# A hybrid encoder block on one core: three changed orders, and the softmax scaling moved from GpSimd to VectorE

## The reference, cut to what matters

```
h    = rms_norm(x) ; q|k|v|p = h @ W_in                   # 512 | 128 | 128 | 512 columns
q, k = rms_norm per head of 64
a    = softmax([q k / 8 over own chunk and the one before (64 + 64 keys), sink]) @ v    # 8 heads, 2 kv heads
m    = trailing means of p over 2, 4, 8, 16 tokens, minus p, then a 128x128 map per group
x    = x + concat([a, m]) @ W_out
x    = x + (silu(gate) * val) @ W_down     # gate|val = causal conv(3) of rms_norm(x) @ W_up, 5632 columns
```

## Time and profile before

| | before |
|---|---|
| median of 3 runs | 1780.61 us |
| the profiled execution's own time | 1780.53 us |
| its span (first to last instruction) | 1778.7 us |
| TensorE busy | 1755.8 us |
| VectorE busy | 1310.2 us |
| ScalarE busy | 782.6 us |
| GpSimd busy | 240.6 us |
| mean granted TensorE clock | 1.000 |
| moved by DMA | 342.70 MB, 193 GB/s on average |

### The profile page before, as it was taken

How to read it: one execution, slowest core, us unless ns; L and a number is a source line. 1 busy time by engine, 2 the same in 40 slices (tenths; PEclk the granted TensorE clock), 3 DMA queues, 4 the chain that set the end, 5 groups by cost and what they waited for, 6 DMA issues and landing times.

```text
span 1778.7 us, 23402 instructions
## 1 busy us (share of the span) xinstructions
PE 1755.8 (99%) x8490; PEld 1462.1 (82%) x8490; DVE 1310.2 (74%) x1772; ACT 782.6 (44%) x1413; POOL 240.6 (14%) x270
## 2 busy tenths in 40 slices
PE   7999999999999999999999999999999999999999
PEld 6888888888878888888888888888888888888887
DVE  5645643533569999999998998998997778865874
ACT  4554543533555444444455444444444433333321
POOL 1213212202100000000000000000003033220210
PEclk9999999999999999999999999999999999999999
DMA  9556584586555623423366223223226999976884
GB/s 329 223 214 221 186 315 178 190 308 237 217 195 181 212 77 107 160 78 97 121 231 230 71 84 95 71 83 95 71 83 230 343 340 334 307 260 211 301 287 130
DMA packets 214243, 342.70 MB, mean 193 GB/s; under 512 B 14377, under 2 KB 106737, under 8 KB 214129
## 3 DMA queue, kind: packets, MB, share of 16 engines
q1 hardware_dynamic: 194702, 288.72, 48.1%
q10 hardware_dynamic: 19427, 52.49, 7.5%
HBM read 262.51 MB, written 78.64 MB: 192 GB/s over the span
## 4 chain that ended last, share of the span: by engine, by line
PE 90%; DVE 4%; DMA 2%; ACT 2%; issue 1%; POOL 0%; ACTq 0%; SPq 0%; DVEq 0%; POOLq 0%
PE ps L805 29%; PE ps L806 29%; PE ps L807 29%; DMA rw<-in_w_up_dram 1%; DVE wv L1734 1%; PE ps L964 1%; PE ps L988 1%; PE ps L975 1%; DMA h2T_d<-n 1%; PE ps L1028 1%; ACT xs L1226 1%; DMA raw<-in_w_in_dram 1%; DVE hT_lo L1556 0%; DVE va_lo L1740 0%; POOL ss_q L2030 0%
## 5 line engine op out<-in xcount | busy, mean ns | idle before, releaser
L805 PE MATMUL ps<-va_hi,wv 128*128 128x512 f32 x1232 | 480.0, 390 | 4.2 <-DVE va_lo L1740 3.2
L807 PE MATMUL ps<-va_hi,wv 128*128 128x512 f32 x1232 | 479.4, 389 | 0.0
L806 PE MATMUL ps<-va_lo,wv 128*128 128x512 f32 x1232 | 479.3, 389 | 0.0
L805 PEld LDWEIGHTS ps<-va_hi,wv 128*128 128x128 f32 x1232 | 231.3, 188 | 54.8 <-issue 4.9
L807 PEld LDWEIGHTS ps<-va_hi,wv 128*128 128x128 f32 x1232 | 231.3, 188 | 47.9
L806 PEld LDWEIGHTS ps<-va_lo,wv 128*128 128x128 f32 x1232 | 231.3, 188 | 47.5
L805 PE MATMUL ps<-dt_hi,ds_hi 128*128 128x512 f32 x616 | 239.8, 389 | 0.0
L806 PE MATMUL ps<-dt_lo,ds_hi 128*128 128x512 f32 x616 | 239.7, 389 | 0.0
L807 PE MATMUL ps<-dt_hi,ds_lo 128*128 128x512 f32 x616 | 239.6, 389 | 0.0
L1823 DVE SCALAR_TENSOR_TENSOR cb<-ub,cst,cb 128x1024 f32<-128x1024 f32 x176 | 218.8, 1285 | 8.5 <-ACT cb L1346 8.5
L1346 ACT ACTIVATE cb<-ub,cst 128x1024 f32<-128x1024 f32 x88 | 109.0, 1243 | 142.5 <-DVE ub L1878 89.5
(11 more groups left out here) (170 smaller groups left out, 2737.6 us busy)
## 6 DMA issues: line engine op xcount, KB each, us to landing
dg<-gT_d SPq DMA_DIRECT2D x264, 256.0 KB, 5.4
rw<-in_w_up_dram SPq DMA_DIRECT2D x84, 512.0 KB, 5.0
dw<-in_w_down_dram SPq DMA_DIRECT2D x132, 256.0 KB, 5.5
w_hi<-wA_d SPq DMA_DIRECT2D x54, 512.0 KB, 3.3
w_lo<-wA_d SPq DMA_DIRECT2D x54, 512.0 KB, 5.1
gT_d<-cb ACTq DMA_DIRECT2D x44, 512.0 KB, 2.6
wA_d<-w_hi SPq DMA_DIRECT2D x18, 512.0 KB, 6.1
wA_d<-w_lo SPq DMA_DIRECT2D x18, 512.0 KB, 7.1
```

What stands on the lines that cost most here:

```text
L805: pe.matmul(out_ap, l_hi, r_hi, start=first, stop=False, skip_group_check=True)
L806: pe.matmul(out_ap, l_hi, r_lo, start=False, stop=False, skip_group_check=True)
L807: return pe.matmul(out_ap, l_lo, r_hi, start=False, stop=last, skip_group_check=True)
```

## The change

Four edits:
1. **Second weight split in the head.** `split(1)` moves from after the fourth `hT` tile of block 0 to after the eighth, on ScalarE and on VectorE.
2. **Third maximum in block 0.** VectorE now does, after `win 0`: the inverse of tile 0, then `s` of tile 2, then the inverse of tile 1, then `s` of tile 3. Before, it did both inverses and then both maxima. The semaphore counts of `sm_step` follow (`SM_S0`, `SM_INV0`).
3. **Fourth product's operand.** A new step `va3` makes `va_hi[3]` and `va_lo[3]` ahead of the last block's norm: on ScalarE ahead of `n2sq`, on VectorE ahead of all four `n2sc_last`.
4. **Scaling of the probabilities.** GpSimd's `inv` is gone; `inverse` on VectorE ends with the same multiplication, so VectorE does it tile by tile, in all four blocks.

```diff
@@ order, block 0
-            units("inv", a, (0,))
+            units("inv1", a, (0,))
             units("pin", a + 1, (2,))
-            units("s", a, (2,), (3,))
+            units("s", a, (2,))
+            units("inv1", a, (1,))
+            units("s", a, (3,))
@@ order, end
     units("o", last, (1, 2), (1, 3))
+    units("va3", last, ())
     units("n2sq", last, ())
@@ ScalarE and VectorE, t1
-                    if a == 0 and i == 3:
+                    if a == 0 and i == KT - 1:
                         split(1)
@@ ScalarE
+            def va3(_):
+                act.wait_ge(S["unit_used"], N_UNITS)
+                v_hi(0, 3)
+                v_hi(1, 3)
             def first_up():
-                act.wait_ge(S["unit_used"], N_UNITS)
-                v_hi(0, 3)
-                v_hi(1, 3)
@@ VectorE
             def inverse(a, t):
...
-                dve.wait_ge(S["sm_step"], 12 * a + SM_INV[t])
+                dve.wait_ge(S["sm_step"], 12 * a + (SM_INV if a else SM_INV0)[t])
                 v.reciprocal(row_sum[:, t, :], row_sum[:, t, :]).then_inc(S["inv_ready"], 1)
+                dve.wait_ge(S["inv_ready"], NT * a + t + 1)
+                pr = xs[:, t, :].rearrange("p (i k) -> p i k", i=8)
+                v.tensor_tensor(pr, pr, row_sum[:, t, :].unsqueeze(2).broadcast_to([P, 8, P]), ALU.mult
+                                ).then_inc(S["p_scaled"], 1)
...
+            def va3(_):
+                v_lo(0, 3)
+                v_lo(1, 3)
             def first_up():
                 n2sc_last(0)
                 n2sc_last(1)
-                v_lo(0, 3)
-                v_lo(1, 3)
                 n2sc_last(2)
                 n2sc_last(3)
@@ GpSimd
-            def inv(a, j):
-                for i in (2 * j, 2 * j + 1):
-                    pool.wait_ge(S["inv_ready"], NT * a + i + 1)
-                    pr = xs[:, i, :].rearrange("p (i k) -> p i k", i=8)
-                    g_.tensor_tensor(pr, pr, row_sum[:, i, :].unsqueeze(2).broadcast_to([P, 8, P]), ALU.mult
-                                     ).then_inc(S["p_scaled"], 1)
```

More of the change, by code:

```diff
@@ L1331, in va @@
                 v_hi(c, i)
+            def va3(_):
+                act.wait_ge(S["unit_used"], N_UNITS)
+                v_hi(0, 3)
+                v_hi(1, 3)
             walk(dict(n1=n1_, n1sq=n1sq, t1=t1, pin=pin, pc=pc, pm=pm, kv=kv, kve=kve, q=q, kt=kt, qt=qt, s=s, pt=pt, av=av,
-                      o=o, n2sq=n2sq, t2=t2, first_weights=first_weights, va=va))
+                      o=o, n2sq=n2sq, t2=t2, first_weights=first_weights, va=va, va3=va3))
             def tap2(un, s):
@@ L1680, in inverse @@
                                 ).then_inc(S["sm_step"], 1)
-                dve.wait_ge(S["sm_step"], 12 * a + SM_INV[t])
+                dve.wait_ge(S["sm_step"], 12 * a + (SM_INV if a else SM_INV0)[t])
                 v.reciprocal(row_sum[:, t, :], row_sum[:, t, :]).then_inc(S["inv_ready"], 1)
+                dve.wait_ge(S["inv_ready"], NT * a + t + 1)
+                pr = xs[:, t, :].rearrange("p (i k) -> p i k", i=8)
+                v.tensor_tensor(pr, pr, row_sum[:, t, :].unsqueeze(2).broadcast_to([P, 8, P]), ALU.mult
+                                ).then_inc(S["p_scaled"], 1)
             SM_S, SM_INV = (0, 2, 6, 8), (5, 6, 11, 12)
+            SM_S0, SM_INV0 = (0, 2, 5, 8), (5, 8, 11, 12)
             def s(a, t):
@@ L1696, in s @@
                                 AX.X, ALU.max).then_inc(S["sm_step"], 1)
-                dve.wait_ge(S["sm_step"], 12 * a + SM_S[t] + 1)
+                first = 12 * a + (SM_S if a else SM_S0)[t]
+                dve.wait_ge(S["sm_step"], first + 1)
                 v.scalar_tensor_tensor(shift[:, t, :], mx[:, t, :], -1.0, neg_sink[:], ALU.mult, ALU.min
                                        ).then_inc(S["sm_step"], 1)
-                dve.wait_ge(S["sm_step"], 12 * a + SM_S[t] + 2)
+                dve.wait_ge(S["sm_step"], first + 2)
                 v.tensor_tensor(sink_exp[:, t, :], sink[:], shift[:, t, :], ALU.add).then_inc(S["shift_ready"], 1)
@@ L1809, in first_weights @@
                     lo(0, i)
-            walk(dict(n1=n1_, n1sc=n1sc, t1=t1, win=win, pin=pin, pl=pl, o=o, q=q, qn=qn, kv=kv, kve=kve, join=join, s=s, inv=inv, av=av,
-                      n2sc=n2sc, first_weights=first_weights, va=va))
+            def va3(_):
+                v_lo(0, 3)
+                v_lo(1, 3)
+            walk(dict(n1=n1_, n1sc=n1sc, t1=t1, win=win, pin=pin, pl=pl, o=o, q=q, qn=qn, kv=kv, kve=kve, join=join, s=s, inv=inv, inv1=inverse, av=av,
+                      n2sc=n2sc, first_weights=first_weights, va=va, va3=va3))
             def tap(un, s, j):
@@ L2084, in _ @@
             pool.wait_ge(const_pool, CONST_POOL)
-            walk(dict(n1=n1sq, n1sq=n1sq, n2sq=n2sq, pin=pin, q=q, kve=kve, inv=inv, av=av))
+            walk(dict(n1=n1sq, n1sq=n1sq, n2sq=n2sq, pin=pin, q=q, kve=kve, av=av))
             def keep_halo(un):
```

## The result

| | before | after |
|---|---|---|
| median (15 runs each) | 1780.64 us (1780.05 to 1782.48) | 1785.06 us (1783.85 to 1787.11) |
| the profiled execution's own time | 1780.53 us | 1784.33 us |
| its span | 1778.7 us | 1782.5 us |

The ratio is 1.0025, with a 95% interval from 1.0018 to 1.0031. The changed kernel is slower by 4.4 us, on the side that the prediction gave a chance of 0.11, and outside its range.

The account below looks back on a forecast made before the run. TensorE, busy 99% of the span, was taken as the bound, so only its waits count. Terms -2.6 - 1.3 + 3.5 + 1.75 = +1.35 on 1780.53 gave 1781.8 us, range 1778.4 to 1783.8.

Parts of the forecast that it names:

- the side that the prediction gave a chance of 0.11: Whole kernel: slower than before by more than 0.2% (3.6 us), chance 0.11.
- The four scalings follow: Switch to the second half: scalings right after the `va_lo` pair, last ending at 518.5; part of edit 3's 2.6 us gain.
- The stream is 1.75 us late: Head: later load of weight unit 3 delays unit 5's landing, so TensorE loses 1.75 us at 38.48.
- no GpSimd pass beside it: Block 0, tile 2's 8-column shift: without GpSimd's multiplication alongside it saves 0.7 us, within the 1.3 us gain.
- The rival by which GpSimd's pass is no hindrance: Block 0: the reorder alone moves tile 2's maximum by 1.0, leaving 0.3 to 0.7 of the wait; 1782.4 us, chance 0.07.
- The landing doesn't move: Head: unit 5 lands as before and edit 1 keeps its 0.8 us gain; 1779.3 us, chance 0.17.
- the page cited in the prediction: Head: skill page's DMA cost, estimated 3.2 us for 512 KB; unit 3 lands no later, edit 1 keeps its gain.
- The `hT_lo` halves don't hold TensorE: Blocks 1 and 2: TensorE has two transposes of probabilities in between, so no 3.5 us loss; 1778.4 us, chance 0.08.
- The gain of edit 3 is given back at 591: TensorE's last wait: if `rw` loads pace its chain, TensorE waits 2.6 us longer there; 1784.5 us, chance 0.09.
- the slower rival: At 591: TensorE arrives 2.6 us earlier but waits that much longer for `rw` loads; 1784.5 us, chance 0.09.
- edit 3's bound of 0: Switch to the second half: worst case for the fourth product's operand, no gain; the other bound was -2.9 us.
- edit 1's +2.7: Head: worst case, unit 5's landing moves by the whole delay of unit 3's load, 2.7 us lost.

Follow-up runs that it names:

- order3: Edit 3 alone (fourth product's operand ahead of the norm) on the kernel before: 1780.21 us against 1780.66, ratio 0.9996.
- order3_psum: Kernel before plus edit 3, its two early `va_lo` passes reading their first input from PSUM: 1779.4 us against 1780.73, ratio 0.9991.
- split1: Edit 1 alone (second weight split after the eighth `hT` tile) on the kernel before: 1784.99 us against 1780.66, ratio 1.0022.
- scale4_late: Kernel before plus edit 4, inverses and scalings of tiles 2 and 3 behind the `hT_lo` halves in blocks 1 and 2: 1781.2 us, ratio 1.0004.
- max2: Edit 2 alone (new order in block 0, GpSimd still scaling) on the kernel before: 1780.03 us against 1780.73, ratio 0.9994.

## Why the prediction was wrong, point by point

**Edit 3: the step that failed.** The prediction has "The four scalings follow (0.7 each); the last waits for GpSimd's power near 517.7 and ends at 518.5". The first half, the fourth product, was right (-1.9 forecast by its idle time and restart, -1.76 to -1.93 measured). The power, however, was taken at the times it had before. Beside the moved `va_lo` pair its two steps for tile 0 grew from 0.19 and 0.55 us to 1.26 and 1.41. Then each scaling holds back the next power (0.55 to 0.91), and the four tiles come one every 1.27 us, where 0.7 was counted. The last scaling ends at 520.82 in `order3`, 2.3 later than forecast; the transposes wait 0.71 us and the fifth product 0.93. So -2.6 was forecast and -0.72 (alone) to -0.80 (in the changed kernel) measured. `order3_psum` recovers 1.2 of the 1.9 us that are missing at the switch in `order3`. The remaining 0.7 is the fifth product's wait, which was to vanish and stays (0.61 us in `order3_psum`, 0.60 before). That the scalings and the powers in turn cause it is inferred from their rows; no run takes it apart. The row that should have told me stood in the trace before: the earlier trace rows show a VectorE instruction of 8 columns held for 0.88 us by a GpSimd pass. I used it for block 0 and did not ask where the same thing would happen the other way round. The same trace had that too: beside the scaling that starts at 515.66, GpSimd's power at 515.91 took 0.91 us in place of 0.55.

**Edit 1: the mechanism was right, its size was off, and an effect was missing.** The load's issue was placed within 0.1 us. The term "The stream is 1.75 us late" is mis-sized: the landing of unit 5 moved by 2.72 us, 2.26 without the later start. The forecast let traffic restart at full rate 1.5 us after the issue; it restarted as a ramp (154 and 256 GB/s in the windows from 22 and 23 us, the first more than 1.3 us after the issue), and the hole is 928 KB. The trace before had shown such a ramp behind the load issued at 13.81: 129 GB/s in the window that the earlier trace rows show, then 267 and 428. What makes the ramp was not tested. Edit 1 cost 2.26 us in the changed kernel's profile and 2.03 alone, against 1.75. Not foreseen at all: after the pause of about 3 us TensorE's clock fell to 1.2 GHz in a share of the runs. It does not show in the changed kernel's profiled execution (clock 1.000). As far as the mean clocks of the runs tell, it is why the median lies at 1785.06 and not near 1784.1, where the seven runs at full clock are. In the profiled execution of `split1` it is 2.7 of 4.9 us.

**Edit 4 in blocks 1 and 2: right.** 1.74 us each were forecast, 1.65 and 1.70 measured, 1.69 and 1.72 alone. `scale4_late` shows the reason given to be the cause: with the same passes behind the halves the loss is gone.

**Edits 2 and 4 in block 0: the sum was right, one reason was not needed.** -1.3 forecast, -1.31 measured. But the 0.7 us by which the shift was to gain from "no GpSimd pass beside it" comes from the order too, since in `max2` the shift falls between two GpSimd passes. The rival by which GpSimd's pass is no hindrance and the reorder leaves 0.3 to 0.7 of the wait has its condition wrong (GpSimd's pass is a hindrance, 0.88 against 0.17 us), and its price too: the reorder alone leaves nothing. Alone, edit 4 makes block 0 worse by 0.28.

**The rivals.** "The landing doesn't move" falls: it moved by 2.26. The same outcome by the page cited in the prediction falls with it. ScalarE's split of unit 3 starts at 25.07, 4.40 us after the load's issue, where the prediction's figure from that page gives 3.2 (an estimate) and the row 6.3. The Trainium skill, DMA: Bandwidth & Descriptors, section Anatomy of one DMA, states that figure for transfers that GpSimd issues. The load here is SyncE's. "The `hT_lo` halves don't hold TensorE" falls: they do. "The gain of edit 3 is given back at 591" falls for the changed kernel: the start there moved by -0.72 more, and kernels that leave the switch alone show between -0.2 and -0.9 at the same place. Its mechanism is half right: the wait is set by an `rw` load, as the idle VectorE in `order3_psum` shows, where it is 0.56 us longer. But the load's issue moves with TensorE, as forecast (574.67 in `order3` against 575.09, -0.42, with TensorE at -0.47 to -0.35 by then), and its duration varies with and without edit 3. The prediction had this wait unchanged; in the changed kernel it is gone, which is luck. The result came out on the slower rival's side, but by another mechanism.

**Sum.** 1.35 forecast; +1.8 from edit 3, +0.5 from edit 1, -0.1 from edit 4, +0.46 at the start and -0.2 at and behind 591 give the 3.8 of the profiles. The 4.4 of the medians holds the spells at the lower clock as well. The range was too narrow because edit 3's bound of 0 and edit 1's +2.7 were each named, but not taken together: with both, the sum is +4.9.

## What to carry to other kernels

When a VectorE pass with two SBUF inputs is moved, list what GpSimd does in its new place as well as what stands behind it in its own queue: a one-column step in a chain through GpSimd can grow by a microsecond. When a load is issued later behind a busy queue, size the hole in bytes and follow it to the last load of the stream; moving the transfer that nobody waits for yet behind the urgent one took the whole loss away here, and no run shows a cost of it. And price a pause of about 3 us on a TensorE that is otherwise busy above its own length: the mean clock was lower in 16 of the 25 runs of the two kernels that have it.

## What the runs showed of the hardware that was not expected

- GpSimd instructions on a 128x1 tile took 1.26 and 1.41 us in place of 0.19 and 0.55 while VectorE ran two passes of 1.2 us with both inputs in SBUF, and 0.19 and 0.55 while it ran passes of the same length with one input in PSUM.
- After TensorE had stood idle for 2.94 us in the middle of a busy stretch, its granted clock was 0.50 from about 41 to 47 us, and the kernel lost about as much again as by the pause (2.7 us). With a pause of the same kind (3.17 us) the changed kernel's profiled execution kept 1.00. Whether a run falls is not settled: 8 of 15 and 8 of 10 did. No run without that pause did: neither the 92 of the kernel before, nor the 110 of the ten kernels without it.
- DMA traffic did not restart at its full rate: behind the load issued at 20.67 the windows of 1 us from 21 us show 37, 154 and 256 GB/s, and from 24 us it is some 407.
- The time from the issue of an `rw` load to VectorE's first use of it was 7.15 to 7.80 us in the four traces where VectorE stood idle for it. With it TensorE's step near 591 varies from -0.9 to +0.5 us over the traces here, as much as some of the edits are worth.
